# Router logits with the router's columns as stationary side, in two column groups, turned back by one product

## What is computed

```python
g_prob = softmax(x @ w_group + b_group)              # (T, 4)
g_p, g_idx = top_k(g_prob, 1)
e_logits = (x @ w_router + b_router).reshape(T, 4, 8)  # (T, 32)
e_logits = take_along_axis(e_logits, g_idx)          # the 8 of the chosen group
e_prob = softmax(e_logits); e_p, e_idx = top_k(e_prob, 2)
weights = g_p * e_p / sum(e_p)
```

## Time and profile before

| what | value |
|---|---|
| median of 3 runs (lowest, highest) | 3594.17 us (3593.21, 3595.28) |
| span of the profiled execution | 3588.6 us |
| own time of the profiled execution beyond its span | not listed; the span is 5.6 us under the median of the runs |
| TensorE busy | 3236.8 us, 90% |
| VectorE busy | 1767.2 us, 49% |
| ScalarE busy | 1272.8 us, 35% |
| GpSimd busy | 1850.7 us, 52% |
| `project_and_route`, layer 0 | from about 605 us to about 878 us of the span |
| `project_and_route`, layer 1 | from about 2717 us to about 2970 us |
| the logits' products, L1100 | 528 records, 67.6 us busy |

### The profile page before, as it was taken

The page is one execution under the profiler, slowest core; times in us unless marked ns, Lnnn a source line. Parts: engine busy times, 40 slices in busy tenths (PEclk is TensorE's granted clock), DMA queues, the critical chain, the costliest instruction groups (busy, mean ns, idle before and its releaser), DMA issues. The chain is left out here.

```text
span 3588.6 us, 57550 instructions
## 1 busy us (share of the span) xinstructions
PE 3236.8 (90%) x20001; PEld 2506.3 (70%) x20001; DVE 1767.2 (49%) x3672; ACT 1272.8 (35%) x2673; POOL 1850.7 (52%) x1443
## 2 busy tenths in 40 slices
PE   6999997996999995997999999999997996999960
PEld 4788885785888884996566666666655876888850
DVE  3555555675443334663555555455534653433316
ACT  2444444222222323443443444444343222223212
POOL 2555553343344432444788888988872223444412
PEclk8999999997999997997999999999998998999975
DMA  2010003543998965886121011022004438999817
GB/s 99 26 39 33 32 33 86 190 152 112 366 317 303 304 210 193 266 267 167 32 51 38 24 51 48 10 51 51 7 13 166 152 123 287 365 320 310 300 65 322
DMA packets 358657, 536.55 MB, mean 150 GB/s; under 512 B 82897, under 2 KB 278773, under 8 KB 351556
## 3 DMA queue, kind: packets, MB, share of 16 engines
q1 hardware_dynamic: 331492, 457.86, 39.8%
q0 software_dynamic: 26976, 76.27, 5.5%
HBM read 397.39 MB, written 145.38 MB: 151 GB/s over the span
## 5 line engine op out<-in xcount | busy, mean ns | idle before, releaser
L2064 POOL TENSOR_TENSOR ab_acc<-ab_acc,ab_pT 128x1024 f32<-128x1024 f32 (+2 forms) x320 | 654.3, 2045 | 136.1 <-ACT ab_pT L2098 103.2
L2098 ACT ACTIVATE ab_pT<-ab_S 128x512 f32<-128x512 f32 (+4 forms) x704 | 376.3, 537 | 574.7 <-PE ab_S L2172 360.3
L2114 DVE TENSOR_REDUCE ab_mx<-ab_W 128x2 f32<-128x1024 f32 (+5 forms) x352 | 347.1, 994 | 400.7 <-PE ab_W L2187 270.7
L1264 POOL DMA_INDIRECT scratch_y<-ex_y,ex_prow x64 | 64.7, 1011 | 490.5 <-issue 353.3
L2221 PE MATMUL ab_O<-ab_pT,ab_v 128*64 128x512 f32 (+4 forms) x1408 | 304.8, 549 | 0.0
L2170 PE MATMUL ab_S<-ab_q_hi,ab_k_hi 97*128 97x512 f32 (+3 forms) x704 | 292.5, 415 | 1.4 <-DVE ab_q_hi L2126 0.7
L1434 PE MATMUL ex_G<-ex_xT,ex_wg 128*128 128x160 f32 x2048 | 291.7, 301 | 2.1 <-DMA ex_wu<-in_moe_w_up 2.1
L1434 PE MATMUL ex_U<-ex_xT,ex_wu 128*128 128x160 f32 x2048 | 288.6, 299 | 0.0
L1434 PEld LDWEIGHTS ex_G<-ex_xT,ex_wg 128*128 128x128 f32 x2048 | 280.0, 190 | 7.3 <-issue 3.6
L1434 PEld LDWEIGHTS ex_U<-ex_xT,ex_wu 128*128 128x128 f32 x2048 | 281.7, 190 | 0.0
L2171 PE MATMUL ab_S<-ab_q_lo,ab_k_hi 96*128 96x512 f32 (+3 forms) x704 | 261.6, 372 | 0.0
(11 more groups left out here) (308 smaller groups left out, 7105.8 us busy)
## 6 DMA issues: line engine op xcount, KB each, us to landing
ex_wg<-in_moe_w_gate SPq DMA_DIRECT2D x64, 1024.0 KB, 7.0
ex_wu<-in_moe_w_up SPq DMA_DIRECT2D x64, 1024.0 KB, 10.9
ex_wd<-in_moe_w_down SPq DMA_DIRECT2D x64, 1024.0 KB, 12.2
pb_y<-scratch_y SPq DMA_DIRECT2D x17, 1024.0 KB, 7.2
pr_o<-scratch_oT SPq DMA_DIRECT2D x33, 512.0 KB, 4.9
scratch_h<-pr_h SPq DMA_DIRECT2D x33, 512.0 KB, 5.0
scratch_xn<-pr_xn SPq DMA_DIRECT2D x33, 512.0 KB, 2.7
fi_y<-scratch_y SPq DMA_DIRECT2D x16, 1024.0 KB, 14.0
```

What stands on the lines that cost most here:

```text
L2064: nc.gpsimd.tensor_tensor(to, to, pT[0:r, U % RING, :, 0:n], ALU.add).then_inc(added, 1)
L2098: nc.scalar.activation(pT[0:r, U % RING, h, 0:n], S[0:r, h, 0:n], ACT.Exp, scale=B_SCALE).then_inc(exped, 1)
L2114: nc.vector.reduce_max(mx[:, :, t, c:c + 1].rearrange("p h a -> p (h a)"), W[:, j % 2, :, 0:n], AX.X).then_inc(emptied, 1)
```

## The change

The sides of the logits' products are exchanged. The 36 router columns become the stationary side and the 128 tokens are streamed, so the result stands with logits on partitions and tokens along the free dimension. Chunks with even number go to partitions 0 to 35 of a new PSUM tile `LT` (column group 0 of the array), those with odd number to partitions 64 to 99 (column group 64): two partial sums. ScalarE copies both to `lgT` in SBUF. One more product, with `lgT` (100 rows) as the stationary side and `pick` as the streamed one, adds the two partials and turns them back to tokens on partitions. `pick` is the sum of two pieces of the identity, made once by GpSimd. The eight products move from the end of the step to the middle of `half(i, 1)`; the one product stands where they stood.

```diff
@@ setup @@
+        pick = s.sb("pick", [P, NL])
+        lgT = s.sb("lgT", [P, P])
+        LT = s.ps("LT", [P, 512])
@@ GpSimd @@
+                nc.gpsimd.memset(lgT[:, :], 0.0)
                 pool.drain().then_inc(zeroed, 1)
-                if first:
-                    pool.wait_ge(early, 16 * NEARLY)
+                pool.wait_ge(early, 16 * NEARLY)
+                nc.gpsimd.tensor_tensor(pick[:, :], ident[:, 0:NL], ident[:, P // 2:P // 2 + NL], ALU.add).then_inc(picked_ready, 1)
@@ ScalarE @@
+                def keep_logits(j):
+                    act.wait_ge(halved, j.count(1, 1))
+                    if j.after(1):
+                        act.wait_ge(scored, j.count(1, 0))
+                    elif j.turn is None:
+                        act.wait_ge(zeroed, 1)
+                    for a in (0, P // 2):
+                        last = nc.scalar.copy(lgT[a:a + NL, :], LT[a:a + NL, 0:P])
+                    last.then_inc(gathered, 1)
                 def step(i):
                     k = i.back(2)
                     if i.turn is None and i.c >= T and i.back(1).live(T):
                         keep_x(i.back(1))
+                        keep_logits(i.back(1))
...
                     if n.live(T):
                         split(n)
+                    if i.live(T) and j.live(T):
+                        keep_logits(j)
                     if i.live(T):
                         act.wait_ge(h_ready, i.count(2, 2))
@@ TensorE @@
-                def half(i, b):
+                def half(i, b, between=None):
...
                     for c in range(DC):
+                        if c == DC // 2 and between is not None:
+                            logit_halves(between)
                         last = products(i, b, c)
...
+                def logit_halves(j):
+                    if j.turn is None and j.c == 0:
+                        pe.wait_ge(consts, 16 * 5)
+                    pe.wait_ge(copied_x, j.count(2, 2))
+                    if j.after(1):
+                        pe.wait_ge(gathered, j.count(1, 0))
+                    for c in range(DC):
+                        a = P // 2 * (c % 2)
+                        last = nc.tensor.matmul(LT[a:a + NL, 0:P], wr[:, c, :], xT[:, c, :], start=(c < 2), stop=(c >= DC - 2),
+                                                skip_group_check=True)
+                    last.then_inc(halved, 1)
                 def logit(j):
                     if j.turn is None and j.c == 0:
-                        pe.wait_ge(consts, 16 * 5)
-                    pe.wait_ge(copied_x, j.count(2, 2))
+                        pe.wait_ge(picked_ready, 1)
+                    pe.wait_ge(gathered, j.count(1, 1))
                     if j.after(1):
                         pe.wait_ge(emaxed, j.count(1, 0))
-                    for c in range(DC):
-                        last = nc.tensor.matmul(LG[:, 0:NL], xT[:, c, :], wr[:, c, :], start=(c == 0), stop=(c == DC - 1))
-                    last.then_inc(scored, 1)
+                    nc.tensor.matmul(LG[:, 0:NL], lgT[0:P // 2 + NL, :], pick[0:P // 2 + NL, :], start=True, stop=True).then_inc(scored, 1)
...
-                        half(i, 1)
+                        half(i, 1, j if j.live(T) else None)
                     k = i.back(2)
                     if i.turn is None and i.c >= T and j.live(T):
+                        logit_halves(j)
                         logit(j)
```

More of the change, by code:

```diff
@@ L771, in project_and_route @@
         copied_x = s.sem("copied_x")
+        halved = s.sem("halved")
+        gathered = s.sem("gathered")
+        picked_ready = s.sem("picked_ready")
         scored = s.sem("scored")
@@ L1091, in _ @@
                 pe.wait_ge(early, 16 * NEARLY)
-                def logit(j):
+                def logit_halves(j):
                     if j.turn is None and j.c == 0:
@@ L1097, in logit @@
                     if j.after(1):
+                        pe.wait_ge(gathered, j.count(1, 0))
[4 more added lines that the diff above has]
+                    last.then_inc(halved, 1)
+                def logit(j):
+                    if j.turn is None and j.c == 0:
+                        pe.wait_ge(picked_ready, 1)
+                    pe.wait_ge(gathered, j.count(1, 1))
+                    if j.after(1):
                         pe.wait_ge(emaxed, j.count(1, 0))
-                    for c in range(DC):
-                        last = nc.tensor.matmul(LG[:, 0:NL], xT[:, c, :], wr[:, c, :], start=(c == 0), stop=(c == DC - 1))
-                    last.then_inc(scored, 1)
+                    nc.tensor.matmul(LG[:, 0:NL], lgT[0:P // 2 + NL, :], pick[0:P // 2 + NL, :], start=True, stop=True).then_inc(scored, 1)
                 def step(i):
```

## The result

The changed kernel takes **3607.14 us** (4 runs, 3606.98 to 3608.37) against 3593.69 us before, measured beside it. The ratio is 1.0042, 95% interval 1.0028 to 1.0057. The forecast was 3610, slower, in a range of 3600 to 3622. Run once more in a later session the changed kernel took 3609.51 us against 3591.3 (1.0051, 1.0035 to 1.0066). Three executions of the two kernels of experiment 4 took 6486, 10400 and 11225 us at granted clocks of 0.98, 0.30 and 0.49 over the whole; why stays open, every ratio leaves them out, and without them the two medians given there would be 3601.2 and 3601.5 us.

The account below looks back on a forecast made before the run. Layer 0 bound by TensorE and a VectorE, ScalarE, GpSimd loop at once, layer 1 by TensorE alone. 1.2 + 17.6 + 1.2 - 5.2 + 0.8 = +15.6 us on 3594.2 gives 3609.8, say 3610; range 3600 to 3622.

Parts of the forecast that it names:

- Two loops at once in layer 0, TensorE alone in layer 1: Layer 0 bound by TensorE (13.84 us) and a VectorE, ScalarE, GpSimd loop (13.83 us); layer 1 by TensorE only.
- Price of the eight products: Inside the second half on TensorE: 16 records in two overlapping column groups, 1.20 us; -0.37 us a step net.
- Rival 2: Column groups do not overlap with 36 columns: the eight products cost 2.1 us, total 3641 us; chance 0.07.
- The stall for `xT`: Layer 0, middle of the second half: TensorE stalls 0.6 us because `eexp` holds ScalarE's copies of `TX`.
- rival 1: ScalarE copies sooner, so no stall on `copied_x`; layer 0 +0.57 us a step, total 3601 us; chance 0.11.
- Layer 0's step of 14.97 to 15.02: From `xn` to `xn` in layer 0: 14.97 us instead of 13.83, taken as +1.17 a step over 15 steps.
- E: Start of the `RK` products, end of `half(i, 1)`; forecast in layer 0 at X + 11.62, X being `xn`'s start on VectorE.
- The first step of a layer, +1.20: First step with the products in its half, no `route` in the way: +1.20 us in each layer.
- Hidden additions: ScalarE's two copies of the partials, 0.28 us each, fall in its wait of over 2 us: no cost.
- The last tile, +0.4 a layer: End of each layer: ScalarE's copies ahead of tile k's exponentials put `place` at 867.6 instead of 867.22, +0.4 us.
- Rival 3: TensorE alone counts in both layers if `xn` shortens by about 1.5 us in layer 0: 3587 us; chance 0.07.
- The distance of 5.6 us between span and time, taken as fixed: Profiled span of 3588.6 us lies 5.6 under the runs' median; added unchanged to reach the forecast time.

Follow-up runs that it names:

- experiment 4: Changed kernel, two separate edits: eight products after 18 instead of 12 products of the half, 3601.39 us; ScalarE's copies of `TX` ahead of tile k's exponentials, 3601.91 us.
- (3): Changed kernel with the eight products back behind the half, their copies behind the sum of squares, the one product in the next step's first half: 3586.99 us.
- (7): Changed kernel, products in old place, layer 0's bias add released by the end of the split: 3582.30 us; last kernel, released by the first `h` add: 3582.89.
- (1): Changed kernel with all eight products in one column group and one partial sum, second copy left out: 3638.46 us, ratio 1.0128.
- (6): Changed kernel with layer 0's bias add at the head of GpSimd's step, released by the end of the split: 3583.66 us, ratio 0.9978.
- (5): Bias add moved behind GpSimd's two scatters: on the changed kernel (first) 3630.08 us, on the kernel before 3599.90, on new products in old place 3595.71.

## Why the prediction was right, step by step

- *Two loops at once in layer 0, TensorE alone in layer 1*: shown. Taking about 0.4 us off TensorE without touching the place (3) moves layer 1's step by 0.43 and layer 0's by 0.04; with the bias add out of VectorE's way as well (7), layer 0 follows too.
- *Price of the eight products, 1.20 us with all changes of shape*: 1.00 from the first record to the next product, against 1.01 in the sum, and 13.50 us for layer 1's step against 13.46. (The prediction's terms add up to 1.21.) The overlap of the groups is shown by (1), +0.87 us without it. Rival 2, at 3641, is close to what (1) measured as its own case: 3638.
- *The stall for `xT`*: named at the right place; the first edit of (4) shows it, and the time of the second fits the cause named, ScalarE's queue behind `eexp`. In the row it is 0.61 us with the change of shape, as forecast. Taking it away gave 0.46 a step: rival 1, which forecast +0.57 a step and 3601 us without the stall, met +0.74 and 3601.4 in (4).
- *Layer 0's step of 14.97 to 15.02*: 15.05. The wait at the second `h` add, 0.8 ahead of `TX`: 1.12 and 0.82 in the rows. In the mean of the steady steps the second add starts at X + 11.80 (forecast 11.82; 10.61 before, where 10.68 was read off half of a merged row), and the way from it to the next X is 3.25 us in both kernels, not 3.15. The terms written out for E add up to X + 11.57, not 11.62, and the step's own to +1.14, not the +1.17 that was taken. The first difference is the 0.06 us between the end of the copies (826.92) and the first record of `LT` (826.98), which no term names; for the second no row was given, and that it went towards the measured 1.19 is luck.
- *The first step of a layer, +1.20*: shown in layer 0 (14.05 to 15.19 us), not in layer 1, where it went from 14.04 to 13.62. The granted clock of these steps differs: 0.94 and 0.95 before, 0.96 and 1.00 after. The changed kernel's second profiled execution has 14.35 us in layer 0 at 1.00. So the close sum of layer 1's stage, -3.9 against -3.6, is in part luck.
- *Hidden additions*: the copies on ScalarE had 3.1 us of room, as said.
- *The last tile, +0.4 a layer*: +0.6, by the mechanism that was forecast, the exponentials behind the copies.
- *Rival 3* put its turning point at `xn` falling to 1.3 us and gave 3587. The kernel of (6) meets its condition and comes near its number: 3584. What the prediction did not see is that `xn` falling is not enough: (5) has `xn` at 1.28 and is 21 to 23 us slower than the change. The cost went to `picked`, ahead of the same `eexp`.
- *The distance of 5.6 us between span and time, taken as fixed*, was wrong: the changed kernel's profiled execution took 3607.1 us with a span of 3605.3, 1.8 apart, and every other listed execution shows 1.8 to 2.2. By 1.8 the profiled execution of the kernel before took about 3590.4 us (an estimate; its own time is not listed), 3.3 under the median of four: it was a quick one. This is why the spans differ by 16.7 us and the medians by 13.5. The sum of +15.6 was 1.1 short of the first and 2.1 over the second. From the true distance the same sum would have given 3606; that 3610 and 3607 lie so close is a balance of two errors.

## What to carry to other kernels

Before moving work on the busiest engine, follow the loop from one tile's last add through the other engines to the next tile's, and see how much room that loop has: work that an engine does outside of it costs its own length once, inside of it it may cost more than it saves elsewhere. Separate the new form of an operation from its new place by one kernel for each; here the form gained about 4 us and the place lost 20, and the place cost next to nothing once the loop was open. Where an operation on VectorE takes longer than the same one elsewhere, look for what GpSimd runs beside it, and move that beside idle time, not beside another operation.

## What was not expected of the hardware

- GpSimd's bias add and the operations of VectorE that it held did not share: the held one ended only after the add had. `picked`, 128x32 with two SBUF inputs, took 3.03 us instead of 0.19 beside a bias add of 2.42 and ended 0.07 us after it; `xn` took 3.4 instead of 1.28 and ended 1.1 after it. It goes the other way too: at the second `xn` of (5), first kernel, `xn` began at 652.94, 0.38 us ahead of the add, and kept its 1.28, and the add took 3.16 instead of 2.4. An add with one input in PSUM kept its 0.69 us beside the bias add. The Trainium skill, SBUF — State Buffer, section SBUF: two separate sides, states this: VectorE and GpSimd share a pair of ports, and whichever starts first holds it for its whole instruction; on VectorE's side that concerns operations in a 2-port mode, and those with two SBUF inputs against a GpSimd operation that reads SBUF. The rows of `xn` and of the `h` add agree. `picked` was held although its record begins 0.54 us ahead of the add's, which these two records leave unexplained.
- Two SBUF inputs are not the whole condition. With one tensor input, the cast of (7) was held, and in early steps of (5), first kernel, so were `ghot` (L999, 128x4: 2.15 us at 682.79 instead of 0.22) and the cast of L1013 (128x2: 1.80 us at 670.64 instead of 0.17), while MAX8 (L990) and the one-column operations of L992 and L998 passed beside the add at their usual lengths. Which operations with one tensor input are held was not tried.
- An idle time of 2.20 us inside an otherwise dense step was followed by 3.4 us at the lower clock level, 1.2 GHz (records of 0.63 us instead of 0.39, granted clock 0.90 over the step); idle times of 0.8 and 0.4 us in one step left it at 1.00 (the changed kernel). Where the clock fell, the stall was paid nearly twice. The length of one idle time alone doesn't decide it: in two steps of the same run 2.27 and 2.21 us left the clock at 1.00, and in two steps of the kernel before with the moved add idle times of 0.62 and 0.61 us were followed by a clock of about 0.90 over the step, while others of 0.61 and 0.66 were not.
- 36 stationary columns in alternate groups run as fast as 64: 16 records in 1.00 us, 8 in 0.59.
